# Attention scores with a 64-row second pass for both heads together, and transposed probabilities copied by ScalarE for head 0 and by VectorE for head 1

## What is computed

```python
def band_attend(q, kb, vb, bias, key_valid):
    s = jnp.einsum('bnthd,bnmhd->bnhtm', q, kb).astype(jnp.float32) * (HEAD_DIM ** -0.5)
    s = s + bias.astype(jnp.float32)[None, None]
    s = jnp.where(key_valid[None, :, None, None, :], s, NEG_INF)
    p = jax.nn.softmax(s, axis=-1).astype(vb.dtype)
    return jnp.einsum('bnhtm,bnmhd->bnthd', p, vb)
```

## Time and profile before

| what | value |
|---|---|
| median of three runs | 2631.17 us |
| the profiled execution's own time | 2631.02 us |
| its span in the trace | 2629.2 us |
| TensorE busy | 2567.8 us, 98% of the span |
| VectorE busy | 1771.9 us, 67% |
| ScalarE busy | 1356.9 us, 52% |
| GpSimd busy | 556.9 us, 21% |

### The profile page before, as it was taken

One profiled execution on the slowest core, in us unless ns is written; L12 is line 12 of the kernel. 1 busy time (PEld: TensorE's weight loads), 2 busy tenths in 40 slices (PEclk: granted clock), 3 DMA queues, 4 the chain that ended last, 5 costly groups with the idle time before them and its releaser, 6 DMA issues.

```text
span 2629.2 us, 49866 instructions
## 1 busy us (share of the span) xinstructions
PE 2567.8 (98%) x18164; PEld 1678.0 (64%) x18164; DVE 1771.9 (67%) x3413; ACT 1356.9 (52%) x2632; POOL 556.9 (21%) x645
## 2 busy tenths in 40 slices
PE   6999899999999999999999999999999999999998
PEld 2466566666666665559986666666666666666665
DVE  5967577587746665566787798888888874242433
ACT  4967374564747773124566555555555553121211
POOL 2600000000017772000001354434333321101000
PEclk8999999999999999999999999999999999999999
DMA  8622513233365432555542445554555449566662
GB/s 294 201 87 88 197 52 137 93 124 133 104 181 122 114 121 107 181 191 148 146 117 86 142 171 176 185 182 157 174 185 180 138 136 349 196 246 233 236 247 95
DMA packets 243890, 424.07 MB, mean 161 GB/s; under 512 B 58424, under 2 KB 163384, under 8 KB 235528
## 3 DMA queue, kind: packets, MB, share of 16 engines
q1 hardware_dynamic: 234872, 413.08, 47.6%
q10 hardware_dynamic: 8848, 8.74, 1.0%
HBM read 284.47 MB, written 139.92 MB: 161 GB/s over the span
## 4 chain that ended last, share of the span: by engine, by line
PE 83%; DVE 5%; ACT 4%; DMA 3%; issue 2%; POOL 2%; SPq 1%; DVEq 0%; ACTq 0%; POOLq 0%
PE ps L3064 55%; PE ps L3319 14%; PE ps L3173 7%; PE ps L3163 2%; PE ps L3145 2%; PE ps L3132 1%; PE ps L3105 1%; POOL arena L1194 1%; ACT arena L1653 1%; DMA arena<-in_w_down 1%; DVE arena L2734 1%; ACT arena L1363 1%; DMA arena<-in_w_mod 1%; ACT arena L1329 1%; DMA arena<-in_w_mod_rest 1%
## 5 line engine op out<-in xcount | busy, mean ns | idle before, releaser
L3064 PE MATMUL ps<-arena 128*128 128x352 f16 (+1 forms) x11880 | 1612.8, 297 | 4.1 <-ACT arena L1821 1.9
L3064 PEld LDWEIGHTS ps<-arena 128*128 128x128 f16 x11880 | 1100.6, 97 | 511.8 <-ACT arena L1821 2.6
L3319 PE MATMUL ps<-arena 128*128 128x352 f16 x2772 | 415.0, 310 | 1.5 <-DVE arena L2763 1.2
L3319 PEld LDWEIGHTS ps<-arena 128*128 128x128 f16 x2772 | 264.7, 96 | 151.8 <-DVE arena L2763 1.5
L1226 POOL TENSOR_TENSOR arena<-arena 128x640 f32<-128x640 f32 (+5 forms) x136 | 150.2, 1123 | 707.5 <-DVE arena L2514 706.1
L1245 POOL TENSOR_TENSOR arena<-arena 128x128 f32<-128x128 f32 x44 | 30.9, 703 | 747.2 <-DMA arena<-in_w_down 746.9
L3173 PE MATMUL ps<-arena 128*128 128x424 f16 (+1 forms) x960 | 171.5, 341 | 0.0
L1813 ACT ACTIVATE arena<-ps 128x352 f32<-128x352 f32 x264 | 116.0, 460 | 94.7 <-PE ps L3064 94.7
L2866 DVE TENSOR_TENSOR arena<-ps,arena 128x352 f32<-128x352 f32 x12 | 6.3, 525 | 204.5 <-PE ps L3319 174.6
L3173 PEld LDWEIGHTS ps<-arena 128*128 128x128 f16 x960 | 92.5, 96 | 78.6
L1446 ACT ACTIVATE arena<-ps 128x352 f32<-128x352 f32 x192 | 80.4, 460 | 118.9 <-PE ps L3064 118.9
(11 more groups left out here) (239 smaller groups left out, 3293.4 us busy)
## 6 DMA issues: line engine op xcount, KB each, us to landing
hidden_combinations<-arena SPq DMA_DIRECT2D x48, 616.0 KB, 3.2
arena<-hidden_combinations SPq DMA_DIRECT2D x24, 1232.0 KB, 7.5
arena<-in_w_up SPq DMA_DIRECT2D x44, 512.0 KB, 5.0
down_combinations<-arena SPq DMA_DIRECT2D x44, 448.0 KB, 2.8
ffn_hidden<-arena SPq DMA_DIRECT2D x44, 440.0 KB, 3.1
arena<-down_combinations SPq DMA_DIRECT2D x10, 1792.0 KB, 7.6
arena<-down_combinations SPq DMA_DIRECT2D x20, 896.0 KB, 6.3
arena<-ffn_hidden SPq DMA_DIRECT2D x50, 352.0 KB, 4.0
```

What stands on the lines that cost most here:

```text
L3064: mm = pe.matmul(out, wt[:, k, wp, :], act_t[:, k, hp], start=(first and k == 0 and n == 0), stop=(last and k == K - 1 and n == 2), skip_g ...
L3319: mm = pe.matmul(ps[:, down_bank(n, k), 0:CF].rearrange("p (w t) -> p w t", w=2), dwt(i)[:, wi, wp, :], dact[i][:, :, bi, hp, :], start=(i ...
```

## The change

Three edits, which need each other only in part.

**The second pass of the scores.** `kll` holds the low key half once: head 0 on partitions 0 to 63, head 1 on 64 to 127, and the second matmul uses only the 64 rows of a head that hold the high half of its query. The product low query x low key is thus left out. `scores` now takes both units of a tile: first both units' first pass (128 rows), then the second pass with the two heads in turn, for 512 columns and then for the rest. `s_filled` of both units is counted on the last matmuls of this second pass.

**The loads.** `kll` is loaded by two transfers per set where there were four, so a set's loads of queries and keys are 10 and not 12, and GpSimd prepares 6 pieces of cached keys per set and not 8.

**The copies.** ScalarE's `probs` copies the first four transposed blocks of head 0 only. Those of head 1 are copied by VectorE, right before its copy of head 1's fifth block. `t_dve` counts both; the waits on TensorE follow.

```diff
@@ the first and second pass, TensorE @@
-            def scores(x):
+            def scores(*units):
+                x = units[0]
                 if x.i == 0:
-                    pe.wait_ge(at_loaded[x.b], 192 * (x.j // 2) + 192)
+                    pe.wait_ge(at_loaded[x.b], 160 * (x.j // 2) + 160)
                 if x.sample:
-                    pe.wait_ge(kc_hi, 8 * x.j + 8)
-                keep_above_zero(pe, s_added, x.u - 1)
-                for bank, c in ((0, min(x.w, 512)), (1, x.w - 512)):
...
+                    pe.wait_ge(kc_hi, 6 * x.j + 6)
+                pieces = [(bank, c, x.k0 + 512 * bank) for bank, c in ((0, min(x.w, 512)), (1, x.w - 512)) if c > 0]
+                q = slice(x.q0, x.q0 + x.rows)
+                for y in units:
+                    keep_above_zero(pe, s_added, y.u - 1)
+                    for bank, c, k in pieces:
+                        pe.matmul(ps[0:x.rows, 2 * y.h + bank, 0:c], qs[x.b][:, y.h, q], khh[x.b][:, y.h, k:k + c],
+                                  start=True, stop=False)
+                for bank, c, k in pieces:
+                    for y in units:
+                        hi = slice(64 * y.h, 64 * y.h + 64)
+                        mm = pe.matmul(ps[0:x.rows, 2 * y.h + bank, 0:c], qs[x.b][hi, y.h, q], kll[x.b][hi, k:k + c],
+                                       start=False, stop=True)
+                        if bank == pieces[-1][0]:
+                            mm.then_inc(s_filled, 1)
@@ the transposes and the outputs, TensorE @@
                 pe.wait_ge(p_scaled, x.u + 1)
-                keep_above_zero(pe, t_act, x.u - 1)
+                if x.h:
+                    keep_above_zero(pe, t_dve, dve_copies(x.u - 1) if x.u > 1 else 0)
+                else:
+                    keep_above_zero(pe, t_act, x.tile)
...
                     if c == 4:
-                        keep_above_zero(pe, t_dve, wide(x.u))
+                        keep_above_zero(pe, t_dve, dve_copies(x.u))
...
-                pe.wait_ge(t_act, x.u + 2)
-                keep_above_zero(pe, t_dve, wide(x.u + 2))
+                pe.wait_ge(t_act, x.tile + 1)
+                pe.wait_ge(t_dve, dve_copies(x.u + 2))
@@ the copies, VectorE @@
+                if x.h == 0 and x.w <= 512:
+                    return
+                G = group_of(x.tile)
+                m, e, c0 = min(4, x.chunks), G.slots(x), x.q0 - G.first.q0
+                dve.wait_ge(t_filled, x.u + 1)
+                keep_above_zero(dve, o_filled, G.n - 1)
+                if x.h:
+                    src = ps[:, 6, 0:m * P].rearrange("p (e n) -> p e n", e=m)
+                    dve.tensor_copy(pt[G.n % 2][1][:, e:e + m, c0:c0 + x.rows], src[:, :, 0:x.rows]).then_inc(t_dve, 1)
                 if x.w > 512:
...
@@ the copies, ScalarE @@
                 if 0 < c <= NTILE:
-                    for h in range(2):
-                        probs(Unit(2 * c - 2 + h))
+                    probs(Unit(2 * c - 2))
@@ the low key halves: layout, loads, cached keys @@
-        kll = [v.rearrange("p (h t) -> p h t", h=2) for v in of_set(4736, 2 * KEYS, F16)]
+        kll = of_set(4736, KEYS, F16)
...
+                for t0, t1, k0 in KEY_PIECES:
+                    sp.dma_start(kll[b][:, k0:k0 + t1 - t0], k_d[j, :, 1, t0:t1]).then_inc(s, 16)
...
-                    pool.tensor_tensor(kll[b][own[h], h, cols], craw[own[h]], khh[b][own[h], h, cols], ALU.subtract)\
+                    pool.tensor_tensor(kll[b][own[h], cols], craw[own[h]], khh[b][own[h], h, cols], ALU.subtract)\
                         .then_inc(kc_hi, 1)
-                    yield
-                for h in range(2):
-                    pool.wait_ge(kc_hi, 8 * j + 4 + 2 * h)
-                    pool.tensor_copy(kll[b][own[1 - h], h, cols], kll[b][own[h], h, cols]).then_inc(kc_hi, 1)
                     yield
```

More of the change, by code:

```diff
@@ L394, in build @@
         w_loaded = [sem(f"w_loaded{i}") for i in range(3)]
-        y_loaded, Y_BASE = (at_loaded[0], at_loaded[1], bias_loaded, kc_loaded), (384, 384, 16 * NJ, 16 * NJ)
+        y_loaded, Y_BASE = (at_loaded[0], at_loaded[1], bias_loaded, kc_loaded), (320, 320, 16 * NJ, 16 * NJ)
         q_filled = sem("q_filled")
@@ L523, in build, with dve_copies @@
         out_cols = ps[:, 7, 0:2 * P]
-        def wide(n):
-            return sum(Unit(k).w > 512 for k in range(n))
+        def dve_copies(n):
+            return sum((Unit(k).w > 512) + Unit(k).h for k in range(n))
         A_ORDER, B_ORDER = (0, 7, 1, 5), (3, 4, 2, 6)
@@ L834, in _ @@
                                  bass.AP(bias_d.tensor, P - 1, [[768, 8], [-1, P], [1, BAND]])).then_inc(band_stored, 16)
+            KEY_PIECES = ((0, TP, 0), (TP, T, TP + PAST))
             def queries_and_keys(j):
@@ L841, in queries_and_keys @@
                         sp.dma_start(qs[b][half, h, :], q_d[j, 64 * h:64 * h + 64, (h + g) % 2]).then_inc(s, 16)
[L842 to L845, removed]
+                    for t0, t1, k0 in KEY_PIECES:
+                        sp.dma_start(khh[b][half, :, k0:k0 + t1 - t0],
+                                     k_d[j, :, 0, t0:t1].rearrange("(h p) t -> p h t", p=64)).then_inc(s, 16)
+                for t0, t1, k0 in KEY_PIECES:
+                    sp.dma_start(kll[b][:, k0:k0 + t1 - t0], k_d[j, :, 1, t0:t1]).then_inc(s, 16)
             def values_and_bias(j):
@@ L856, in cached_keys @@
                 if j:
-                    sp.wait_ge(kc_hi, 8 * j)
+                    sp.wait_ge(kc_hi, 6 * j)
                 sp.dma_start(craw, a["cache_kT"][j]).then_inc(kc_loaded, 16)
@@ L1202, in cached_halves @@
                 pool.wait_ge(kc_loaded, 16 * j + 16)
-                keep_above_zero(pool, kc_hi, 8 * j)
+                keep_above_zero(pool, kc_hi, 6 * j)
                 if j >= 2:
@@ L1232, in _ @@
                 for h in range(2):
-                    keep_above_zero(pool, kc_hi, 8 * j + min(8, max(0, i - 4)))
+                    keep_above_zero(pool, kc_hi, 6 * j + min(6, max(0, i - 4)))
                     scaled(Unit(2 * c + h))
-                if 4 <= i < 12:
+                if 4 <= i < 10:
                     pool.wait_ge(p_scaled, 2 * c + 2)
@@ L2501, in probs @@
             def probs(x):
-                if x.w > 512:
[L2504 to L2508, removed]
+                if x.h == 0 and x.w <= 512:
[7 more added lines that the diff above has]
+                    dve.tensor_copy(pt[G.n % 2][1][:, e:e + m, c0:c0 + x.rows], src[:, :, 0:x.rows]).then_inc(t_dve, 1)
+                if x.w > 512:
+                    k, e = min(P, x.w - 512), (e + 4) % 5
+                    dve.tensor_copy(pt[G.n % 2][x.h][0:k, e, c0:c0 + x.rows], ps[0:k, 5, P * x.h:P * x.h + x.rows])\
+                        .then_inc(t_dve, 1)
             def inverse_sums(x):
@@ L3184, in _ @@
                 if c < NTILE:
-                    scores(Unit(2 * c))
-                    scores(Unit(2 * c + 1))
+                    scores(Unit(2 * c), Unit(2 * c + 1))
                 for G in parts_in(c):
```

2 lines of the change are left out of this document (1 added, 1 removed).

## The result

| | before | changed |
|---|---|---|
| median of six runs | 2631.78 us | 2641.66 us |
| range | 2630.45 to 2632.91 | 2639.25 to 2642.72 |
| ratio | | 1.0038 (1.0026 to 1.0050) |
| span of the profiled execution | 2629.2 us | 2638.3 us |

The changed kernel is 9.9 us slower, 0.38%. The forecast was 14.7 us slower, 2645.7, with a range of 2635 to 2653.

What follows compares the result with a forecast made beforehand. TensorE was taken to bound full tiles, but not the first four or the sample tile. Per set +1.5 (full tiles), +1.6 (tiles 1 to 4) and +0.5 (sample), 14.7 over four sets, gave 2645.7 us, range 2635 to 2653.

Steps and rivals of the forecast that it cites:

- What bounds the kernel: Attention stage: TensorE alone bounds full tiles, 3.74 us a cycle; in the first four tiles and sample it does not.
- Second pass, 0.27 saved if the halves run at once: TensorE's scores: two heads on different row halves overlap, so the second pass costs 0.27 us, not 0.55.
- Change of shape, 0.14: TensorE's cycle: a third array shape adds one more change, costing 0.14 us.
- Scores ready 0.41 later: TensorE to VectorE: head 0's scores are ready 1.16 us after scores start, 0.41 later than before.
- The copy, 0.69, and 0.61 of the queue: VectorE: copying 128 x 512 float32 from PSUM takes 0.69 us and moves its queue by 0.61.
- "Worth nothing" for ScalarE's copy: ScalarE: losing a 590 ns copy per cycle gains nothing, as it stood idle 0.82 us afterwards.
- The chain of 3.94: VectorE in full cycles: its chain with the new copy takes 3.94 us where `out_hi` is included, otherwise 3.66.
- Tile 1: VectorE's chain in this narrow tile: 1.79 + 0.21 for the copy of tile 0, 2.00 us.
- TensorE's path of 3.84: Every second full cycle: TensorE's outs wait for VectorE's last copy, and the path to the next scores takes 3.84 us.
- "faster": Rival for the attention: the copy does not lengthen VectorE's chain and TensorE takes its 3.60; 6 us gained, 2625; chance 0.07.
- "half price": Rival for VectorE's copy: it runs at twice the slope, 0.43 us; 2636; chance 0.12, with unseen chain slack.
- "No overlap": Rival for TensorE's scores: row halves run one after another, path grows 0.27; +6 us, 2652; chance 0.12.

Runs made afterwards that it cites:

- run 7: The changed kernel with VectorE's copies of head 1's blocks put ahead of head 1's reciprocal; 2643.08 us, 1.0046 of the kernel before.
- run 6: The kernel before with head 0's fifth transposed block put in PSUM bank 1 in place of bank 5; 2622.97 us, 0.9969 of before.
- run 5: The changed kernel with both heads' second pass on rows 0 to 63, for timing only as scores are wrong; 2649.93 us, 1.0070 of the kernel before.
- run 1: The changed kernel with both copies back on ScalarE, so the new second pass alone; 2636.99 us, 1.0020 of the kernel before.
- run 3: The changed kernel with VectorE's copy of head 1's blocks done twice in three of four sets; 2670.27 us, 1.0147 of the kernel before.
- run 2: The kernel before with head 1's four blocks copied by VectorE, scores untouched; 2639.71 us, 1.0034 of before.
- run 4: The changed kernel with the second pass ordered head 0 (512, 128), then head 1 (512, 128); 2644.13 us, 1.0048 of the kernel before.

## Why the prediction was right in kind and half again too large

The forecast was +14.7 and the result +9.9: slower as forecast, inside the range, and at the low edge of the forecast's own 2641 to 2649. Term by term:

- **What bounds the kernel**: right. Tiles 1 to 4 by VectorE's chain (in run 7 they fall from 10.94 to 9.98 when the copy leaves it), full tiles by TensorE (run 6).
- **Second pass, 0.27 saved if the halves run at once**: right (run 5: 0.27). **Change of shape, 0.14**: about right, 0.11 by run 5, so 0.16 net for 0.13. TensorE's shorter queue shows in the cycles of 3.57 of run 1, but over the whole kernel it brought no time, there or in the change.
- **Scores ready 0.41 later**: measured 1.14 us (881.71 to 882.85) for 0.75, so 0.39. Run 1 shows what follows: the attention is 4.6 us longer although TensorE's own work is 0.16 a cycle less.
- **The copy, 0.69, and 0.61 of the queue**: 0.690 measured, 0.607 from its start (885.820) to the next; run 3 shows 0.60 for one more.
- **"Worth nothing" for ScalarE's copy**: wrong in one place, tile 0. There the outs waited for ScalarE's copies, and started 0.54 us behind the bias addition of head 0 (889.72); now they start 0.18 behind it (894.15), with ScalarE's one copy over at 893.71 and VectorE's last at 894.23 (so it is VectorE that they wait for, though the row names ScalarE). Before, then after:

```profile
890.26 2.40 PE L3163 MATMUL ps<-arena 128*64 128x256 f32 x24 [0.57 <-ACT arena L1664]
```

```profile
894.33 2.39 PE L3177 MATMUL ps<-arena 128*64 128x256 f32 x24 [0.91 <-ACT arena L1663]
```

The outs come 0.36 earlier, VectorE's copy further on in the tile costs 0.2 (from the copy of the fifth block to tile 1's bias addition, 893.14 to 894.03 before and 897.20 to 898.30 now), and tile 0 is 0.16 shorter where it was forecast unchanged. **Loads, cached keys**: nothing contradicts "nothing"; they were not tried by themselves.
- **The chain of 3.94, the mis-sized term.** It measured 3.79. Piece by piece, with the forecast in brackets (882.85 to 886.63): scores to exponential 0.86 (0.86), exponential to exponential 1.09 (1.11), to the reciprocal 0.94 (0.98), reciprocal to copy 0.08 (0.17), copy 0.61 (0.61), last block 0.21 (0.21). More than half of the 0.15 too much lies in the 0.17. It was read at 881.97 to 882.14, where the copy could not start before TensorE's last transposes (they end at 882.10); it was a wait, taken for the instruction's own time. In the changed kernel the transposes end 0.37 us before the copy starts, and it follows the reciprocal at 0.08. The trace of before had a place that ran free, in the cycle of tile 6:

```profile
852.26 0.17 DVE L2514 RECIPROCAL arena<-arena 128x1 f32<-128x1 f32 x1 [0.38 <-ACT arena L1653]
852.34 0.29 DVE L2508 COPY arena<-ps 128x128 f32<-128x128 f32 x1
```

The same excess stood in tiles 2, 3, 4 and the sample tile (2.36 for 2.48; 2.85 for 2.97; 3.59 for 3.73; 3.61 for 3.77).
- **Tile 1**: 2.13 for 2.00, a term that was too small, so tiles 1 to 4 together came out nearer to the forecast than tiles 2, 3 and 4 by themselves. Its cycle also has ScalarE's short output copy (0.12 us from start to start), which the sum left out.
- **TensorE's path of 3.84** measured 3.86, and in its pieces too: landing 0.38 (0.33), outs 1.24 (1.24), transposes to VectorE's copy 0.80 (0.81), to the next scores 0.51 (0.51), to readiness 1.14 (1.16), less 0.20 (0.21).
- **The sum**: 2.6 us a set for 3.67, so four sets are some 10.5 us longer, and the attention is 10.8. In the two profiles the rest of the kernel happens to be 1.7 us shorter with the change (1.2 ahead of the attention, 0.5 behind it), so the profiled executions differ by 9.1; the medians differ by 9.9.
- **Rivals**: "faster" falls with runs 1 and 2, "half price" with the 690 ns. "No overlap" had its price right, 6 us (run 5), but the halves do overlap.

## To carry to other kernels

Where engines hand one tile from one to the next in a ring, add up the ring for each kind of tile, with every instruction that stands in order between the last wait and the next tile; the slower of that and the busiest engine's queue is the cycle. Taking work off the busiest engine can lose if its result comes later for the others, and a free engine has no room at a place where its own queue is the ring. In such a sum an interval from start to start is the instruction's own only if nothing else was awaited there: look for a second place where it ran free.

## What the runs showed of the hardware

- Two matmuls on different halves of the rows start 3 to 4 ns apart in the trace of the change, and the pair takes about one's time (0.45 us for four matmuls, against 0.71 when all are on one half). By the starts in run 4, TensorE does this over an instruction of the first half that stands between them in program order, and the time from scores to outs stays at 1.02 us. The Trainium skill, TensorE: Matmul & The Clock Gate, "The mechanism", gives about 4 ns between such starts, which agrees; it also says that matmuls are not reordered, and the starts in run 4 differ from it.
- A wait of 0.11 us between two transposes cost 0.17 a cycle: without it the piece went from 1.41 to 1.24, as the scores behind the delayed transpose also started 0.06 later (run 6).
- Going from 128 rows to 64 rows for the second pass, one shape of the array more in a cycle, cost 0.11 us (run 5: 1.29 against 1.18).
- VectorE's copy of 128 x 512 float32 from PSUM takes 0.69 us, and the next instruction starts 0.607 us behind its start.
- In run 3 the granted clock fell to a mean of 0.66 for 5 us, a mixture of its two levels of 2.4 and 1.2 GHz; in the stretch ahead TensorE had been busy 2.76 of 4 us. The same waits in the second set of that trace left it at 1.00, so what set it off is not shown. With the change itself it was 1.00 in the set shown; from 775 to 780 and 780 to 785 us, at the start of the attention, it was 0.58 and 0.73 with the change, and 0.77 and 0.89 before.
